# Merged recurrence and gather on TensorE: token transposes in pairs, their use two slots behind

## The chip, the cores and the metric

One core of a Trainium2 chip runs the whole program in one launch. The metric is the time of an execution in microseconds (us) of device time. The kernel before takes 2057.97 us, the median of three runs (2055.84 to 2064.03).

## What is computed

One inference step of a hybrid decoder layer, over a prompt of 1024 tokens and eight sampled sequences with a paged cache of 2048 rows each. Three token mixers stand side by side: a gated linear attention (GLA), a sparse attention with compressed, selected and window branches, and an mLSTM. The stage that is changed does two jobs of it. The first is the GLA recurrence over the prompt:

```python
# S_t = diag(a_t) S_{t-1} + k_t^T v_t,  o_t = q_t S_t, evaluated chunk by chunk
rel = jnp.where(causal, bcum[:, :, :, None, :] - bcum[:, :, None, :, :], -jnp.inf)
scores = jnp.einsum('bhtd,bhsd,bhtsd->bhts', qc, kc, jnp.exp(rel))
o = einsum('bhts,bhse->bhte', scores, vc) + einsum('bhtd,bhde->bhte', qc * exp(bcum), s)
s_new = exp(b_end) * s + einsum('bhsd,bhse->bhde', kc * exp(b_end - bcum), vc)
```

The second prepares the sampled sequences: for each of the eight, the cached rows are gathered through the page table, and every 16 rows of compression keys and values go through the first layer of an MLP (`r @ w1`), and the selection keys are multiplied by the queries.

## The kernel before, in words

The program is a row of stages, each a block in which every engine has its own instruction stream and engines wait for each other on semaphores. The stage of the change is `gla_and_gather` (line 1528), which runs from about 771 to 1036 us. Its order is written out by hand. It loops `it` over eight iterations (`NCH` = 8 chunks of 128 prompt tokens, and at the same time `NS` = 8 sequences), and a short ninth one finishes chunk 7. An iteration has 12 slots `n` (`NFILL`).

What TensorE issues, all in float32:

- `fill(s, n)` (line 1676): four 128x128 transposes of gathered rows of sequence s into PSUM bank `TP[n % 2]`. It waits until the copy of slot n-2 has emptied that bank. For slots 0 and 6 it waits for the gather too.
- The copy out of that bank to `tr[:, n % 4]` is done by ScalarE for slots 0, 2, 4, 5, 6, 7, 8, 10 (line 1776) and by VectorE for 1, 3, 9, 11 (line 1867).
- `use(s, n)` reads what was copied. In slots with n % 6 below 4 it is eight matmuls on 64 rows with the MLP's weights (line 1692, called **use** below); in slots 4, 5, 10, 11 it is four matmuls on 128 rows with only 8 moving columns, the queries (line 1700, called **short use** below). Use 0 of a sequence waits for `hid_ready`: ScalarE copies the sums of the sequence before (`copy_hidden`, lines 1781 and 1782, after its use 11), then VectorE adds to them (`add_hidden`, line 1873).
- `level(c, l)` (line 1717), l from 0 to 7: four matmuls on 64 rows that give one level of chunk c's scores. There is one pair of PSUM banks for them, so level l waits (`sc_used`) until VectorE's `merge` of level l-1 (lines 1848 and 1849) has taken the scores over. Level 0 waits in addition for `queries` of VectorE.
- `turn_keys` (line 1725), `keys_by_values` (line 1731) and `outputs` (lines 1741 and 1743). `outputs` waits for all eight merges.

Before, TensorE takes slot after slot: fill n, then in slots 6 to 11 level n-6 (in slots 0 and 1 levels 6 and 7 of the chunk before), then use n-1. `outputs` of the chunk before stands in slot 3, `turn_keys` in slot 5, `keys_by_values` in slot 8.

VectorE's order matters: after the copy of slot 3 it does `update` (line 1857, needs `outputs`), `queries` (lines 1831 to 1837), the `differences` for the next chunk (lines 1820 to 1825), and then merge 0. In slot 1 it does the copy, `add_hidden`, merge 7. ScalarE has, beside its copies, two exponent passes per chunk. GpSimd multiplies keys and issues the gathers; SyncE stores gathered values to DRAM.

The code of the loop:

```python
for n in range(NFILL if it < NCH else 4):
    if it < NCH:
        fill(it, n)
    if n < 2 and it:
        level(it - 1, n + 6)
    if n >= 6 and it < NCH:
        level(it, n - 6)
    if n and it < NCH:
        use(it, n - 1)
    elif n == 0 and it:
        use(it - 1, NFILL - 1)
```

Of the kernel before, what the change touches and what calls it, by code (L numbers as in the profile page):

```python
# [67 lines left out]
NCH = T // CH  # L68
# [1459 lines left out]
def gla_and_gather(nc, io, keep, at):  # L1528
# [6 lines left out]
    with ExitStack() as ctx:  # L1535
# [22 lines left out]
        NFILL = 12  # L1558
# [3 lines left out]
        def copies(s, n):  # L1562
            own = by_act if n in by_act else by_dve
            return len(own) * s + own.index(n) + 1
# [12 lines left out]
        with nc.Block() as block:  # L1577
# [88 lines left out]
            def _(pe):  # L1666
                def fill(s, n):
                    half, f = n // 6, n % 6
                    if f == 0:
                        pe.wait_ge(gathered[half], 16 * (s + 1))  # L1670
                    if NFILL * s + n >= 2:
                        prior = (s, n - 2) if n >= 2 else (s - 1, n + NFILL - 2)
                        pe.wait_ge(copied_a if prior[1] in by_act else copied_v, copies(*prior))
                    for u in range(4):
                        token = kv[half][:, (f % 2) * 4 + u, f // 2, :, :].rearrange("p h d -> p (h d)")
                        last = nc.tensor.transpose(TP[n % 2][:, u * P:(u + 1) * P], token, ident[:, :])
                    last.then_inc(f_done, 1)

                def use(s, n):
                    half, f = n // 6, n % 6  # L1680
                    pe.wait_ge(copied_a if n in by_act else copied_v, copies(s, n))
                    if f < 4:
                        j = f // 2
                        if n == 0:
                            pe.wait_ge(w_in, 16)
                            if s:
                                pe.wait_ge(hid_ready, s)
                        for u in range(4):
                            r = half * 8 + (f % 2) * 4 + u
                            for h in range(2):  # L1690
                                rws = slice(h * 64, h * 64 + 64)
                                last = nc.tensor.matmul(HID[h][:, j, :], w1[rws, j, r, :, :].rearrange("d w e -> d (w e)"),
                                                        tr[rws, n % 4, u * P:(u + 1) * P],
                                                        start=(j == 0 and r == 0), stop=(h == 1 and j == 1 and r == 15))
                    else:
                        if n == 4:
                            pe.wait_ge(gated, 1)
                        for u in range(4):
                            r = half * 8 + (f - 4) * 4 + u
                            last = nc.tensor.matmul(SCP[:, r * 8:r * 8 + 8], tr[:, n % 4, u * P:(u + 1) * P], qbd[:, s, :],  # L1700
                                                    start=False, stop=r == 15)
                    last.then_inc(f_used, 1)

                def level(c, l):
                    if l == 0:
                        if c == 0:
                            pe.wait_ge(setup, 1)
                        pe.wait_ge(keyed, c + 1)
                        pe.wait_ge(queried, c + 1)
                    if 8 * c + l:  # L1710
                        pe.wait_ge(sc_used, 8 * c + l)
                    for hp in range(HP):
                        for side in range(2):
                            rws = slice(side * 64, side * 64 + 64)
                            k, q = ((zq[rws, c % 2, 2 + hp, :], zq[rws, c % 2, hp, :]) if l == NL else
                                    (kd[c % 2][rws, hp, l, :], dd[c % 2][rws, hp, l, :]))
                            last = nc.tensor.matmul(side_sc[:, side, hp, :], k, q, start=True, stop=True)
                    last.then_inc(sc_done, 1)

                def turn_keys(c):  # L1720
                    pe.wait_ge(keyed, c + 1)
                    if c:
                        pe.wait_ge(g_updated, c)
                    for hp in range(HP):
                        last = nc.tensor.transpose(kt[:, hp * P:(hp + 1) * P], kd[c % 2][:, hp, KEND, :], ident[:, :])
                    last.then_inc(kt_done, 1)

                def keys_by_values(c):
                    pe.wait_ge(kt_copied, c + 1)
                    for hp in range(HP):  # L1730
                        last = nc.tensor.matmul(dl[:, hp * P:(hp + 1) * P], kn[:, hp, :], vnat[:, c, hp * P:(hp + 1) * P],
                                                start=True, stop=True)
                    last.then_inc(dl_done, 1)

                def outputs(c):
                    pe.wait_ge(sc_used, 8 * c + 8)
                    if c:
                        pe.wait_ge(og_copied, c)
                        pe.wait_ge(g_updated, c)
                    for h in range(4):  # L1740
                        nc.tensor.matmul(og[:, h * 64:(h + 1) * 64], pT[:, h % 2, h // 2, :], vnat[:, c, h * 64:(h + 1) * 64], start=(h == 0), stop=False)
                    for hp in range(HP):
                        last = nc.tensor.matmul(og[:, hp * P:(hp + 1) * P], dd[c % 2][:, hp, QIN, :], G[:, hp, :],
                                                start=False, stop=hp == HP - 1)
                    last.then_inc(og_done, 1)

                for it in range(NCH + 1):
                    for n in range(NFILL if it < NCH else 4):
                        if it < NCH:
                            fill(it, n)  # L1750
                        if n < 2 and it:
                            level(it - 1, n + 6)
                        if n >= 6 and it < NCH:
                            level(it, n - 6)
                        if n and it < NCH:
                            use(it, n - 1)
                        elif n == 0 and it:
                            use(it - 1, NFILL - 1)
                        if n == 3 and it:
                            outputs(it - 1)  # L1760
                        if n == 5:
                            turn_keys(it)
                        if n == 8:
                            keys_by_values(it)

            @block.scalar
# [1584 lines left out]
```

## Time and profile before

| | |
|---|---|
| median of three runs | 2057.97 us (2055.84 to 2064.03) |
| the profiled execution, its own time | 2060.44 us |
| its span, first to last instruction | 2058.7 us |
| TensorE matmuls busy | 1810.5 us, 88% |
| VectorE busy | 1115.2 us, 54% |
| ScalarE busy | 636.6 us, 31% |
| mean granted TensorE clock | 0.923 of full speed |

The profile is one execution recorded by the hardware. The 1.7 us between its time and its span lie outside the instructions. The granted clock has two levels: 1.00 is 2.4 GHz and 0.50 is 1.2 GHz; a stretch that holds both shows a value between. In the timeline a row is a run of instructions of one line; a matmul here leaves two records, a transpose one. Ends of matmuls are modelled, so spacings from start to start are the safer measure.

### The profile page before, as it was taken

To read this page: it belongs to the slowest core of one execution; us is meant where nothing else is said; L and a number is where in the kernel's file an instruction comes from. 1 tells how busy PE (TensorE), PEld (TensorE's weight loads), DVE (VectorE), ACT (ScalarE), POOL (GpSimd) and SP (SyncE) were. 2 spreads that over 40 slices of the span, in tenths; PEclk is the share of its full clock that TensorE was granted. 3 is DMA by queue.
4 is the path that set the end of the run, shared out by engine and by line. 5 is a ranking of instruction groups with operands and counts; after the bars stand their busy time and mean duration, and the time that the engine had idled before them with its cause. 6 is when DMAs were issued, how large, how long until landed. Compare 5 with 4: busy or idle time off the path is not lost. (4 is left out here: it accounts for less than half of the span.)

```text
span 2058.7 us, 32209 instructions
## 1 busy us (share of the span) xinstructions
PE 1810.5 (88%) x12919; PEld 1679.4 (82%) x12919; DVE 1115.2 (54%) x1984; ACT 636.6 (31%) x1136; POOL 118.4 (6%) x141
## 2 busy tenths in 40 slices
PE   6989999667888886889974478999999999999997
PEld 5989989656676775777863278999999999999997
DVE  5462662266777663555555765744445544444544
ACT  6513322144554443333223334512121111121111
POOL 0000000000000004132112120000000000000000
PEclk8989999858999997999976679999999999999999
DMA  7631143410000005554464547211111111211102
GB/s 189 87 95 32 52 154 122 112 23 21 11 12 1 1 2 219 191 175 179 140 164 66 174 154 217 77 39 59 41 41 41 41 41 43 79 41 41 41 21 83
DMA packets 172273, 170.87 MB, mean 83 GB/s; under 512 B 49788, under 2 KB 156884, under 8 KB 168452
## 3 DMA queue, kind: packets, MB, share of 16 engines
q1 hardware_dynamic: 168692, 131.54, 22.2%
q0 software_dynamic: 2304, 33.56, 4.3%
q10 hardware_dynamic: 1168, 4.26, 0.9%
q8 instruction: 75, 1.23, 0.3%
q14 instruction: 34, 0.28, 0.0%
HBM read 136.98 MB, written 36.56 MB: 84 GB/s over the span
## 5 line engine op out<-in xcount | busy, mean ns | idle before, releaser
L58 PE MATMUL pm<-hidH,weights 128*128 128x344 f32 x768 | 247.2, 322 | 4.4 <-DVE weights L3166 4.4
L58 PE MATMUL pm<-hH,wuH 128*128 128x344 f32 x768 | 247.1, 322 | 3.1 <-DVE wuL L3161 3.1
L59 PE MATMUL pm<-hidL,weights 128*128 128x344 f32 x768 | 246.3, 321 | 0.0
L60 PE MATMUL pm<-hidH,weights 128*128 128x344 f32 x768 | 246.0, 320 | 0.0
L60 PE MATMUL pm<-hH,wuL 128*128 128x344 f32 x768 | 245.7, 320 | 0.0
L59 PE MATMUL pm<-hL,wuH 128*128 128x344 f32 x768 | 245.6, 320 | 0.0
L58 PE MATMUL pz<-hH,winH 128*128 128x344 f32 x600 | 202.2, 337 | 11.0 <-DVE zb L830 6.5
L59 PE MATMUL pz<-hL,winH 128*128 128x344 f32 x600 | 195.7, 326 | 0.0
L60 PE MATMUL pz<-hH,winL 128*128 128x344 f32 x600 | 195.5, 326 | 0.0
L3170 DVE SCALAR_TENSOR_TENSOR act<-pm,onat 128x344 f32<-128x344 f32 x96 | 49.3, 516 | 245.9 <-PE pm L60 245.7
L3181 DVE TENSOR_TENSOR onat<-pm,onat 128x344 f32<-128x344 f32 x256 | 129.0, 513 | 70.3 <-PE pm L60 70.3
L58 PEld LDWEIGHTS pm<-hidH,weights 128*128 128x128 f32 x768 | 144.8, 189 | 4.7 <-issue 4.7
L58 PEld LDWEIGHTS pm<-hH,wuH 128*128 128x128 f32 x768 | 144.9, 189 | 3.9 <-issue 3.3
L59 PEld LDWEIGHTS pm<-hidL,weights 128*128 128x128 f32 x768 | 145.2, 189 | 0.0
L60 PEld LDWEIGHTS pm<-hidH,weights 128*128 128x128 f32 x768 | 145.0, 189 | 0.0
L60 PEld LDWEIGHTS pm<-hH,wuL 128*128 128x128 f32 x768 | 145.0, 189 | 0.0
L59 PEld LDWEIGHTS pm<-hL,wuH 128*128 128x128 f32 x768 | 144.6, 188 | 0.2
L58 PEld LDWEIGHTS pz<-hH,winH 128*128 128x128 f32 x600 | 116.5, 194 | 15.0 <-issue 13.5
L1362 ACT ACTIVATE pm<-pS,nm 128x640 f32<-128x640 f32 (+7 forms) x128 | 89.5, 701 | 122.4 <-DVE nm L1439 122.4
L3048 ACT ACTIVATE act<-act 128x1032 f32<-128x1032 f32 x32 | 34.1, 1067 | 280.5 <-DVE act L3170 280.5
L3044 ACT ACTIVATE weights<-hs 128x2048 fp32r<-128x2048 f32 x16 | 30.7, 1919 | 286.3 <-PE pm L60 286.3
L59 PEld LDWEIGHTS pz<-hL,winH 128*128 128x128 f32 x600 | 116.3, 194 | 0.9
(592 smaller groups left out, 3556.4 us busy)
## 6 DMA issues: line engine op xcount, KB each, us to landing
uact<-in_w_up_dram SPq DMA_DIRECT2D x16, 1024.0 KB, 6.8
hs<-in_w_down_dram SPq DMA_DIRECT2D x16, 1024.0 KB, 4.9
raw<-in_w_in_dram SPq DMA_DIRECT2D x24, 512.0 KB, 3.9
vS_scratch<-page_rows SPq DMA_DIRECT2D x16, 512.0 KB, 4.8
hold<-vS_scratch SPq DMA_DIRECT2D x8, 1024.0 KB, 12.9
wo<-in_w_out_dram SPq DMA_DIRECT2D x12, 512.0 KB
act<-in_w_out_dram SPq DMA_DIRECT2D x12, 512.0 KB, 3.9
onat<-qkT_scratch SPq DMA_DIRECT2D x18, 256.0 KB, 4.1
```

The source lines that it names most:

```text
L58: nc.tensor.matmul(out, wH, mH, start=(k == 0), stop=False)
L59: nc.tensor.matmul(out, wH, mL, start=False, stop=False)
L60: last = nc.tensor.matmul(out, wL, mH, start=False, stop=(k == n - 1))
L1362: nc.scalar.activation(pm[:, u % 2, g, at:at + w], bank[:, 0:w], ACT.Exp, bias=nm[:, s % 4, 0:1], accum_out=den[:, u % 2, g, branch - 1:br ...
L3044: nc.scalar.activation(wdH[:, :, :], wd[:, :, :], ACT.Copy).then_inc(wdH_ready, 1)
L3048: nc.scalar.activation(act2[:, f, :], act2[:, f, :], ACT.Square)
L3170: nc.vector.scalar_tensor_tensor(out=act2[:, f, cols[third]], in0=ps[third][:, 0:TC], scalar=0.0, in1=rn[:, cols[third]], op0=ALU.max, op1 ...
L3181: nc.vector.tensor_tensor(y, ps[4 + n % 4][:, 0:TC], y, ALU.add).then_inc(added, 1)
```

## The change

TensorE alone gets another order; no instruction is added or taken away, and no other engine's stream is touched. Slots are taken in pairs (0 and 1, 2 and 3, and so on): both fills of the pair come first, into both banks; then level, use, level, use, and the use is that of the slot two behind. `outputs` follows slot pair 2, `turn_keys` pair 4, `keys_by_values` pair 8.

```diff
-                    for n in range(NFILL if it < NCH else 4):
+                    for first in range(0, NFILL if it < NCH else 4, 2):
                         if it < NCH:
-                            fill(it, n)
-                        if n < 2 and it:
-                            level(it - 1, n + 6)
-                        if n >= 6 and it < NCH:
-                            level(it, n - 6)
-                        if n and it < NCH:
-                            use(it, n - 1)
-                        elif n == 0 and it:
-                            use(it - 1, NFILL - 1)
-                        if n == 3 and it:
+                            fill(it, first)
+                            fill(it, first + 1)
+                        for n in (first, first + 1):
+                            if n < 2 and it:
+                                level(it - 1, n + 6)
+                            if n >= 6 and it < NCH:
+                                level(it, n - 6)
+                            if n >= 2 and it < NCH:
+                                use(it, n - 2)
+                            elif n < 2 and it:
+                                use(it - 1, NFILL - 2 + n)
+                        if first == 2 and it:
                             outputs(it - 1)
-                        if n == 5:
+                        if first == 4:
                             turn_keys(it)
-                        if n == 8:
+                        if first == 8:
                             keys_by_values(it)
```

How TensorE's instructions stand, at two places. `page_rows` are gathered rows (fill), `prs` the scores (level), `w_heads` the MLP weights (use), `qbd_n` the queries (short use).

First place, levels 0 to 2 of chunk 1. Before, from `turn_keys` on:

```order
L1725 MATMUL pr<-ident,kd 128x128 x2
L1676 MATMUL pr<-ident,page_rows 128x128 x4
L1717 MATMUL prs<-hold,kd 128x128 x4
L1700 MATMUL pr<-qbd_n,hs 128x8 x4
L1676 MATMUL pr<-ident,page_rows 128x128 x4
L1717 MATMUL prs<-hold,kd 128x128 x4
L1692 MATMUL pr<-hs,w_heads 128x128 x8
L1676 MATMUL pr<-ident,page_rows 128x128 x4
L1717 MATMUL prs<-hold,kd 128x128 x4
L1692 MATMUL pr<-hs,w_heads 128x128 x8
```

With the change:

```order
L1725 MATMUL pr<-ident,kd 128x128 x2
L1676 MATMUL pr<-ident,page_rows 128x128 x8
L1717 MATMUL prs<-hold,kd 128x128 x4
L1700 MATMUL pr<-qbd_n,hs 128x8 x4
L1717 MATMUL prs<-hold,kd 128x128 x4
L1700 MATMUL pr<-qbd_n,hs 128x8 x4
L1676 MATMUL pr<-ident,page_rows 128x128 x8
L1717 MATMUL prs<-hold,kd 128x128 x4
L1692 MATMUL pr<-hs,w_heads 128x128 x8
L1717 MATMUL prs<-hold,kd 128x128 x4
L1692 MATMUL pr<-hs,w_heads 128x128 x8
```

Both fills of slots 6 and 7 now stand ahead of level 0, and only the short use 4 stands between level 0 and level 1; behind level 1 come a short use and eight transposes, where before a full use followed at once.

Second place, around the end of a sequence: levels 6 and 7, use 11, use 0 and `outputs`. Before:

```order
L1676 MATMUL pr<-ident,page_rows 128x128 x4
L1717 MATMUL prs<-hold 128x128 x4
L1700 MATMUL pr<-qbd_n,hs 128x8 x4
L1676 MATMUL pr<-ident,page_rows 128x128 x4
L1717 MATMUL prs<-zq 128x128 x4
L1692 MATMUL pr<-hs,w_heads 128x128 x8
L1676 MATMUL pr<-ident,page_rows 128x128 x4
L1692 MATMUL pr<-hs,w_heads 128x128 x8
L1676 MATMUL pr<-ident,page_rows 128x128 x4
L1692 MATMUL pr<-hs,w_heads 128x128 x8
L1741 MATMUL pr<-hold,pTg 128x64 x4
L1743 MATMUL pr<-Gst,hold 128x128 x2
```

With the change:

```order
L1676 MATMUL pr<-ident,page_rows 128x128 x8
L1717 MATMUL prs<-hold 128x128 x4
L1700 MATMUL pr<-qbd_n,hs 128x8 x4
L1717 MATMUL prs<-zq 128x128 x4
L1700 MATMUL pr<-qbd_n,hs 128x8 x4
L1676 MATMUL pr<-ident,page_rows 128x128 x8
L1692 MATMUL pr<-hs,w_heads 128x128 x16
L1741 MATMUL pr<-hold,pTg 128x64 x4
L1743 MATMUL pr<-Gst,hold 128x128 x2
```

Use 11, the last short one, now stands behind level 7; between it and use 0 there are the eight transposes of slots 2 and 3, and uses 0 and 1 run together just ahead of `outputs`.

## Rows read from the trace of the kernel before

**Rows 1.** Page, part 1: busy time, share of the span, instructions.
```profile
PE 1810.5 (88%) x12919; PEld 1679.4 (82%) x12919; DVE 1115.2 (54%) x1984; ACT 636.6 (31%) x1136; POOL 118.4 (6%) x141
```

**Rows 2.** Windows, the merged stage; columns: PE, PEld, DVE, ACT, POOL busy, granted clock, DMA.
```profile
790.50:1032.70 242.20, 217.19 (x2300) 187.81 (x2300) 129.69 (x298) 78.98 (x116) 51.18 (x21) 0.94 0.47 162
```

**Rows 3.** Waits of TensorE, 775 to 1035 us: in total, times, longest.
```profile
PE prs L1717 <- DVE pTg L1849: 10.7, 7, 1.7
...
PE pr L1692 <- DVE onat L1873: 7.9, 7, 1.1
PE prs L1717 <- issue: 4.1, 7, 0.6
```

**Rows 4.** Timeline, TensorE, 811 to 852 us: start, duration, line, count, idle before.
```profile
818.78 1.68 PE L1692 MATMUL pr<-hs,w_heads 64*128 64x128 f32 x16 [1.12 <-DVE onat L1873]
...
823.70 1.16 PE L1692 MATMUL pr<-hs,w_heads 64*128 64x128 f32 x16
824.79 1.10 PE L1741 MATMUL pr<-hold,pTg 128*128 128x64 f32 x8
825.74 0.66 PE L1743 MATMUL pr<-Gst,hold 128*128 128x128 f32 x4
...
830.60 0.72 PE L1717 MATMUL prs<-hold,kd 64*128 64x128 f32 x8 [0.58 <-issue]
...
834.48 0.71 PE L1717 MATMUL prs<-hold,kd 64*128 64x128 f32 x8 [1.68 <-DVE pTg L1849]
835.02 1.06 PE L1692 MATMUL pr<-hs,w_heads 64*128 64x128 f32 x16
...
842.88 0.66 PE L1676 MATMUL pr<-ident,page_rows 128*128 128x128 f32 x4
843.47 0.72 PE L1717 MATMUL prs<-hold,kd 64*128 64x128 f32 x8
844.11 1.06 PE L1700 MATMUL pr<-qbd_n,hs 128*128 128x8 f32 x8
845.03 0.63 PE L1676 MATMUL pr<-ident,page_rows 128*128 128x128 f32 x4
...
846.24 1.06 PE L1700 MATMUL pr<-qbd_n,hs 128*128 128x8 f32 x8
...
849.55 1.71 PE L1692 MATMUL pr<-hs,w_heads 64*128 64x128 f32 x16 [1.12 <-DVE onat L1873]
```

**Rows 5.** Timeline, VectorE, the same stretch.
```profile
817.78 0.86 DVE L1873 TENSOR_TENSOR onat<-pr,onat 64x254 f32<-64x254 f32 x2
...
826.44 1.16 DVE L1857 SCALAR_TENSOR_TENSOR Gst<-Gst,eb,pr 64x64 f32<-64x64 f32 x4 [1.94 <-PE pr L1743]
...
833.70 0.72 DVE L1849 COPY_PREDICATED pTg<-lvl,prs 128x512 f32<-128x512 uint32 x1
```

**Rows 6.** Timeline, ScalarE, the same stretch.
```profile
816.56 0.77 ACT L1781 ACTIVATE onat<-pr 64x256 f32<-64x256 f32 x2 [1.04 <-PE pr L1700]
```

**Rows 7.** Windows with the granted clock, columns as in rows 2.
```profile
815.90:819.20 3.30, 2.18 (x25) 1.85 (x26) 2.48 (x6) 1.03 (x3) 3.14 (x2) 1.00 0.00 0
819.20:822.70 3.50, 3.50 (x30) 2.95 (x28) 0.41 (x1) 0.60 (x1) 0.04 (x1) 0.51 0.76 253
...
829.50:834.50 5.00, 2.74 (x27) 2.17 (x25) 4.75 (x12) 1.47 (x3) 0.96 (x1) 1.00 0.82 221
```

**Rows 8.** Windows with the granted clock, end of the stage.
```profile
1027.40:1030.80 3.40, 2.94 (x30) 2.52 (x29) 1.34 (x3) 1.02 (x3) 0.00 (x0) 1.00 0.00 0
1030.80:1034.50 3.70, 1.77 (x9) 1.77 (x9) 1.72 (x4) 0.01 (x1) 0.00 (x0) 0.51 0.00 0
```

**Rows 9.** Timeline, TensorE, start of the stage.
```profile
790.55 2.08 PE L1692 MATMUL pr<-hs,w_heads 64*128 64x128 f32 x16 [8.37 <-DMA w_heads<-w1S_scratch]
```

**Rows 10.** Timeline, TensorE, end of the stage.
```profile
1028.02 0.72 PE L1717 MATMUL prs<-hold,kd 64*128 64x128 f32 x8
...
1029.65 0.71 PE L1717 MATMUL prs<-zq 64*128 64x128 f32 x8
```

## The prediction, made before the changed kernel ran

> **What bounds the kernel now.** I read the page first: TensorE is busy for 88% of the span [rows 1], but that is a mean over all stages. The change touches one, so I read the windows of that stage next: 242.2 us, of which TensorE's matmuls are busy for 217.2, VectorE for 129.7, ScalarE for 79.0, at a granted clock of 0.94 [rows 2]. TensorE bounds it, except where its waits stand. The list of waits puts these down to two places per iteration [rows 3]: merge 0 of a chunk (10.7 us in 7 waits, with 4.1 us more ahead of level 0), and `add_hidden` (7.9 us in 7). The timeline then gives one iteration in full [rows 4], and the windows the clock [rows 7, 8].
>
> One iteration lasts 30.77 us (use 0 at 818.78 and again at 849.55). I cut it into four pieces, from start to start:
>
> 1. End of `outputs` (825.74 + 0.66 = 826.40) to level 1 (834.48): 8.08 us [rows 4]. VectorE sets this: its `update` starts at 826.44 and merge 0 ends at 833.70 + 0.72 = 834.42 [rows 5], one thing behind the other. TensorE idles 0.58 + 1.68 = 2.26 us in it.
> 2. Level 1 to use 11 (846.24): 11.76 us, all of it TensorE's own work.
> 3. Use 11 to use 0 (849.55): 3.31 us. ScalarE starts its copies 1.09 us after use 11 (816.56, a cycle earlier) [rows 6], `add_hidden` runs from 817.78 to 818.64 [rows 5], and use 0 starts 0.14 us later. TensorE idles 1.12 us.
> 4. Use 0 to the end of `outputs` (818.78 to 826.40): 7.62 us, of which part runs at the low clock.
>
> The clock is the fourth cost. Soon after use 0 the granted clock falls: 1.00 from 815.9 to 819.2, then 0.51 from 819.2 to 822.7 [rows 7], that is, the 1.2 GHz level for nearly all of it. At full clock piece 4 up to `outputs` would be three uses at 1.09 (823.70 to 824.79) and two fills at 0.59 (842.88 to 843.47), 4.45 us, where the trace has 6.01. So the fall costs 1.56 us, and 10.9 us over the seven iterations that have it. At full clock an iteration would last 29.21 us.
>
> **The change part by part, cycle of 29.21 us.** No instruction is added or removed and only TensorE's order changes, so the costs are waits, switches and the clock.
>
> Piece 1: VectorE's chain starts at the end of `outputs` and has the same links, so level 1 still starts 8.08 us after it. On TensorE both sides of the piece hold four fills, three uses, `turn_keys` and level 0; with the second fill ahead of level 0, the 0.58 us wait there goes, and the one ahead of level 1 grows to about 2.1 us. **Zero.**
>
> Piece 2: it takes in one fill (0.59), one level (0.64) and one short use (0.92) [rows 4]: +2.15 us. Added too is waiting inside the pairs. Now only a use stands between two levels. The nearest row is the end of the stage, where it is so already: level 6 to level 7 takes 1.63 us [rows 10], against 0.64 + 0.92 = 1.56 us of work, so +0.07 us for each of four pairs, 0.28. The lower bound is nothing; the upper is 0.69 more per pair where VectorE's own copy gets between two merges, which its order puts behind the first of them. Against that stand fewer changes between 64-row and 128-row work: 11 round trips per iteration now, 8 then. The row gives use after fill 1.09 us, use after level about 0.99 (835.02 and the fill behind it), so 0.10 us each, −0.3 us. The Trainium skill says that changing the tiling mode drains TensorE (TensorEngine Tiling (Array Packing), Key Properties), with no figure; the sum goes by the row's 0.10. Piece 2 becomes 13.9 us.
>
> Piece 3: ScalarE's copies and `add_hidden` follow use 11 as before; the cover changes from fill 1 and level 7 to fills 2 and 3, both about 1.15 us. VectorE's copy of slot 1 is now done earlier, which frees about 0.06. So 3.25 us, wait about 1.2. Merge 7 still stands behind `add_hidden` on VectorE, but `outputs` comes two uses later: covered.
>
> Piece 4: two fills and one use move out (2 x 0.59 + 1.09 = 2.27), and use 1 directly behind use 0 saves one switch: 6.06 − 2.37 = 3.69 us at full clock.
>
> Sum: 8.08 + 13.95 + 3.25 + 3.69 = about 29.0 us, −0.2 us per iteration, −1.4 in seven. The ends: in iteration 0, fills 2 and 3 move into the 8.37 us wait for the weights [rows 9] and the wait for merge 0 there goes (0.5 us); at the stage's end use 11 stands one level (0.64) later and the last `outputs` waits for it. Together −1.2 us. **Order alone: −2.6 us.**
>
> **The clock** decides the rest, and the trace shows the new situation only in parts. What came before a fall: at 819.2, short uses and levels and then 1.12 us of idling; at 1030.8, short uses and levels with hardly any idling, TensorE busy for 2.94 of 3.40 us, and yet 0.51 afterwards [rows 8]. What came before none: 829.5 to 834.5, with 2.3 us idle, stayed at 1.00 [rows 7]; there a fill stands between the short use and the long wait, and a full use follows at once. With the change short use 4, a wait of 2.1 us, level 1 and short use 5 are neighbours, and in each iteration level, short use, level, short use stand in a row as at the end of the stage. I expect a fall at merge 0's wait in every iteration, dearer than nothing and at most the 1.56 us of today, since part of the slow stretch lies in the wait: 1.4 us, 9.8 in seven. At use 0 a wait of 1.2 us remains; the fall there comes in about four iterations of seven, 1.3 us each, 5.2. That makes 15.0 us, where 10.9 are lost now: +4.1. Bounds: 7 (one cheap fall per iteration) and 21.8 (two full ones), −3.9 and +10.9.
>
> Total −2.6 + 4.1 = **+1.5 us**. The profiled execution's own time, 2060.44 us, would become 2062; it stands 2.5 us above the median of the runs, so against the median 2058.0 I say **2059.5 us**. Other stages keep their instructions; a stage that starts at another moment may lose or gain a clock stretch of the same 1.5 us, which I add to the range.
>
> **Rivals.**
>
> *The falls go away.* The iteration loses its regular 30.77 us, the fills cover the waits, and the clock stays up. Time 2058.0 − 2.6 − 10.9 = 2044.5 us. For it: longer waits than 1.12 us already pass without a fall [rows 7]. Against it: the 2.1 us wait now has light work on both sides.
>
> *The falls multiply.* Level, short use, level, short use, then fills, then a wait: the clock falls there, again at merge 0's wait, and once it is low a weak stretch keeps it low, 2.5 stretches of 1.56 us per iteration, 27.3 us: 2058.0 − 2.6 + 16.4 = 2072 us. It passes 0.5% from about 3.3 us lost per iteration on. For it: the fall at 1030.8 after exactly this pattern [rows 8]. Against it: between 790.5 and 1032.7 the mean clock is 0.94, one fall an iteration, and every low stretch in the cycle ended after one. The Trainium skill speaks for it: transposes, it says, do not bring TensorE to the full clock, as they do not count as busy in the same way (TensorE: Matmul & The Clock Gate, Part 4). By that rule eight in a row would cost as much as idling, and the time would be this rival's. The trace does not bear it out: eight transposes and 2.3 us of idling lie between 829.5 and 834.5 at 1.00.
>
> *The merges become the bound.* If VectorE's copies of slots 1, 9 and 11 each push a merge by 0.69 us that TensorE waits for, seven or eight iterations pay 2.1 us: +15 us, 2073 us. Against it: the copies stand behind the merge that is waited for first.
>
> *Nothing changes* (one fall per iteration at another place) is inside the forecast.
>
> **How the numbers follow.** A measurement of this kernel can tell about 0.5%, 10.3 us, from no change. The forecast gets 0.74 and all of it lies within 0.5%; falls gone 0.12, faster; falls multiplied 0.10 and merges 0.04, slower. Its own bounds are 2058.0 − 2.6 − 3.9 = 2051.5 and 2066.3; other stages and the spread of runs (6 us above the median, 2 below) widen them, and the range reaches some way to both rivals: 2047 to 2070 us.
>
> **What would show it.** Right: `outputs` to level 1 still 8.1 us with one wait of about 2.1; no wait at level 0; levels in a pair 1.6 us apart; use 11 to use 0 3.25 us; iterations of 29 us where no fall lies, 30.5 where one does; a low stretch behind level 1. Wrong: iterations of 29 throughout (first rival), a mean clock under 0.90 in the stage (second), gaps over 2 us from level to level (third), or VectorE's chain itself of another length.

## The result, and the profile of the changed kernel

| | before | changed |
|---|---|---|
| median of nine runs | 2055.56 us (2049.70 to 2064.03) | 2070.55 us (2066.14 to 2080.90) |
| profiled execution's own time | 2060.44 us | 2068.03 us |
| its span | 2058.7 us | 2066.3 us |

The ratio is 1.0081 with a 95% interval of 1.0062 to 1.0100: the changed kernel is 15 us slower. My forecast was no change, 2059.5 us, with a range up to 2070.0; the rival "the falls multiply" had been put at 2072 us and a chance of 0.10. The two profiled executions lie 7.6 us apart, not 15: that of the kernel before took 4.9 us more than its median, that of the changed kernel 2.5 us less.

TensorE on the page, against [rows 1]; then the changed kernel's windows, the first over the whole stage as in [rows 2] (from the first use to the last `outputs`), the others over one iteration. The columns are busy time of PE, PEld, DVE, ACT and POOL, granted clock, DMA share, GB/s:

```profile
PE 1829.7 (89%) x12919; PEld 1703.5 (82%) x12919; DVE 1112.5 (54%) x1984; ACT 634.3 (31%) x1136; POOL 117.9 (6%) x141
```

```profile
788.50:1038.40 249.90, 227.56 (x2292) 206.00 (x2292) 121.77 (x292) 75.87 (x115) 51.08 (x21) 0.85 0.45 156
...
823.40:826.80 3.40, 1.81 (x17) 1.52 (x16) 3.23 (x12) 1.07 (x3) 0.91 (x1) 1.00 0.92 256
826.80:833.60 6.80, 6.12 (x36) 5.56 (x38) 1.49 (x5) 2.10 (x2) 0.42 (x1) 0.50 0.81 308
833.60:847.20 13.60, 12.40 (x150) 11.10 (x148) 6.60 (x17) 5.34 (x8) 5.51 (x2) 1.00 0.09 20
847.20:850.60 3.40, 3.40 (x33) 3.18 (x32) 1.23 (x2) 0.00 (x0) 0.00 (x0) 0.51 0.93 390
```

The stage takes 249.9 us where it took 242.2, at a mean clock of 0.85 where it was 0.94. TensorE's matmuls are busy 10.4 us longer in the stage with the same instructions. Within the iteration shown the clock is at 0.50 from 826.8 to 833.6, twice as long as the low stretch of an iteration before, and again from 847.2 to 850.6. Low time in the whole stage is 76 us, where it was 31. It lies in two places per iteration: a stretch of 3.4 us around use 0 in all seven, and one around level 1 in all seven too, of 6.8 us in six of them and 3.4 in the last. In the kernel before there was only the one at use 0. In these six the fall comes by turns 0.7 us ahead of the start of level 1, inside the wait, and 0.6 us behind it; at use 0 it comes 0.2 us behind the start, or 2.1 us ahead of it, before the wait has begun.

The waits of TensorE, against [rows 3], and its timeline over one iteration, against [rows 4]:

```profile
PE prs L1717 <- DVE pTg L1851: 13.0, 6, 2.2
...
PE pr L1692 <- DVE onat L1875: 5.5, 7, 1.2
```

```profile
818.75 0.66 PE L1743 MATMUL pr<-Gst,hold 128*128 128x128 f32 x4
...
822.47 1.04 PE L1676 MATMUL pr<-ident,page_rows 128*128 128x128 f32 x8
823.61 0.71 PE L1717 MATMUL prs<-hold,kd 64*128 64x128 f32 x8
824.26 1.06 PE L1700 MATMUL pr<-qbd_n,hs 128*128 128x8 f32 x8
827.49 1.22 PE L1717 MATMUL prs<-hold,kd 64*128 64x128 f32 x8 [2.17 <-DVE pTg L1851]
828.64 1.87 PE L1700 MATMUL pr<-qbd_n,hs 128*128 128x8 f32 x8
830.36 1.95 PE L1676 MATMUL pr<-ident,page_rows 128*128 128x128 f32 x8
832.24 1.23 PE L1717 MATMUL prs<-hold,kd 64*128 64x128 f32 x8
...
843.20 0.71 PE L1717 MATMUL prs<-zq 64*128 64x128 f32 x8
843.85 1.06 PE L1700 MATMUL pr<-qbd_n,hs 128*128 128x8 f32 x8
844.76 1.07 PE L1676 MATMUL pr<-ident,page_rows 128*128 128x128 f32 x8
847.03 3.62 PE L1692 MATMUL pr<-hs,w_heads 64*128 64x128 f32 x32 [1.20 <-DVE onat L1875]
850.59 1.13 PE L1741 MATMUL pr<-hold,pTg 128*128 128x64 f32 x8
```

Read it by the pieces of the prediction. End of `outputs` (818.75 + 0.66 = 819.41) to level 1 at 827.49 is 8.08 us, as before; the wait ahead of level 1 is 2.17 us and there is none ahead of level 0 (823.61). Around it stand short use, wait, level, short use, transposes, and there the rows nearly double: short use 828.64 to 830.36 takes 1.72 us instead of 0.92, eight transposes 1.88 instead of 1.0. Use 11 (843.85) to use 0 (847.03) is 3.18 us. From use 0 to `outputs` two uses take 3.56 us (to 850.59); at full clock they would take about 2.0.

### The profile page after: what moved, and what is told of

Same layout as the page of the kernel before. It is cut to its first block and busy times, and to the rows that moved or that the text cites. A ratio compares the mean times of both kernels' runs of the same rounds, so it can differ in the third digit from the quotient of the medians.

```text
span 2066.3 us, 32209 instructions
## 1 busy us (share of the span) xinstructions
PE 1829.7 (89%) x12919; PEld 1703.5 (82%) x12919; DVE 1112.5 (54%) x1984; ACT 634.3 (31%) x1136; POOL 117.9 (6%) x141
## 5 line engine op out<-in xcount | busy, mean ns | idle before, releaser
L58 PEld LDWEIGHTS pz<-hH,winH 128*128 128x128 f32 x600 | 115.9, 193 | 15.0 <-issue 13.5
```

The lines of the kernel that those rows point to most:

```text
L58: nc.tensor.matmul(out, wH, mH, start=(k == 0), stop=False)
```

## The experiments

Twelve kernels ran, ten of them variants and two the kernels themselves once more. "Stage" is the time from the first use to the start of the last `outputs` in the profiled execution, "low" the time in it at the 1.2 GHz level, "ratio" that of the runs to those of the kernel before on the same chip (whose medians there were 2057.1 to 2058.5 us for e1 to e10, 2055.56 us for the changed kernel). "Profiled" is the time of the execution that stage and low are read from; it can lie some us off the median, and stages are rounded by themselves. Where the text says by how many us a kernel beats the changed one, the two medians can be from different chips; the ratios are the safer measure.

| kernel | median, us | ratio (95%) | profiled, us | stage, us | low, us |
|---|---|---|---|---|---|
| before | 2055.56 | | 2060.44 | 242.2 | 31 |
| changed | 2070.55 | 1.0081 (1.0062 to 1.0100) | 2068.03 | 249.9 | 76 |
| e1 changed, waits fed | 2047.80 | 0.9949 (0.9931 to 0.9967) | 2050.82 | 230.0 | 15 |
| e2 before, waits fed | 2056.73 | 0.9991 (0.9978 to 1.0003) | 2050.07 | 235.1 | 13 |
| e3 single slots, use two behind | 2076.49 | 1.0091 (1.0075 to 1.0107) | 2082.84 | 266.0 | 82 |
| e4 pairs, use one behind | 2055.86 | 1.0006 (0.9992 to 1.0020) | 2055.64 | 237.7 | 26 |
| e5 short uses together | 2043.19 | 0.9926 (0.9909 to 0.9943) | 2049.45 | 229.3 | 48 |
| e6 changed, fed with transposes | 2046.81 | 0.9958 (0.9946 to 0.9971) | 2048.06 | 229.5 | 18 |
| e7 e5 with its wait fed | 2041.15 | 0.9926 (0.9911 to 0.9941) | 2041.75 | 218.8 | 11 |
| e8 changed, fed elsewhere | 2086.82 | 1.0158 (1.0131 to 1.0186) | 2082.05 | 267.3 | 66 |
| e9 changed, merge 0 first | 2043.78 | 0.9925 (0.9910 to 0.9939) | 2045.62 | 233.1 | 52 |
| e10 e5, merge 0 first | 2037.27 | 0.9900 (0.9885 to 0.9915) | 2037.27 | 217.8 | 30 |
| c1 before, once more | one execution | | 2059.75 | 243.3 | 35 |
| c2 changed, once more | one execution | | 2062.75 | 251.3 | 77 |

**The theory**: the order itself is no slower; the loss is TensorE's clock, which falls where waits and light work (short uses, levels) stand together. **The rival**: the new order costs by itself, in waits or in its spacing.

### Feed the waits with idle matmuls

```diff
+def warm(n):
+    for _ in range(n):
+        nc.tensor.matmul(og[:, 256:384], ident[:, :], ident[:, :], start=True, stop=True)
...
+warm(7)    # ahead of level 1, iterations 1 to 7
 level(it, 1)
...
+warm(4)    # ahead of use 0
 use(it, 0)
```

> The changed kernel, with idle matmuls of TensorE (a product of the identity with itself into the unused half of the outputs' bank, read by nobody) put into its two waits: seven ahead of level 1, four ahead of use 0, in iterations 1 to 7. They add 11 matmuls per iteration, about 1.9 and 1.1 us, less than the waits of 2.17 and 1.2 us. Clock theory (the changed kernel loses 3.4 us per iteration to the 1.2 GHz level, because light work stands around its waits): the low stretches go, iterations come down from 32.4 us to 29 to 30 us, the time falls by 16 to 24 us against the changed kernel, to 0.5% below the kernel before or better. Rival (the new order itself costs: levels too close, use behind use, a longer chain): the clock stays up but the time stays within 5 us of the changed kernel or rises.

The windows of the stage and the timeline around level 1:

```profile
790.70:1020.70 230.00, 222.06 (x2447) 200.95 (x2447) 122.78 (x294) 75.88 (x115) 49.15 (x21) 0.97 0.50 171
```

```profile
856.12 1.06 PE L1700 MATMUL pr<-qbd_n,hs 128*128 128x8 f32 x8
857.04 1.81 PE L1706 MATMUL pr<-ident 128*128 128x128 f32 x14
859.36 0.72 PE L1721 MATMUL prs<-hold 64*128 64x128 f32 x8 [0.51 <-DVE pTg L1860]
860.00 1.06 PE L1700 MATMUL pr<-qbd_n,hs 128*128 128x8 f32 x8
```

It came out as the theory says: 2047.80 us, 22.8 us under the changed kernel (ratios 0.9949 and 1.0081) and 0.5% under the kernel before, with 11 more matmuls in each of seven iterations. The stage is 19.9 us shorter at a clock of 0.97. The feed (857.04) lies where the wait was; what is left of it is 0.51 us, and the short use and the fills behind level 1 run at their full-clock times again. Iterations without a low stretch last 28.53 us from `outputs` to `outputs`. So this is what the new order takes at full clock.

In two of the seven iterations a low stretch of 3.4 us is left, and no wait stands ahead of it. The windows ahead of one, and over it:

```profile
869.70:873.90 4.20, 4.20 (x42) 3.76 (x41) 1.38 (x4) 0.60 (x1) 4.05 (x2) 1.00 0.00 0
873.90:877.30 3.40, 3.40 (x18) 3.40 (x17) 1.91 (x5) 1.52 (x4) 0.88 (x1) 0.50 0.53 159
```

Ahead of it stand eight transposes, level, short use, level, short use, with TensorE busy for all of the 4.20 us, and the clock falls all the same. So the theory needs one correction: this work can bring a fall without a wait, here in two iterations of seven. In the changed kernel the fall at use 0 came in all seven, in three of them ahead of the wait too (878.0, 942.8 and 1007.7).

The same in the kernel before (two ahead of level 0, five ahead of level 1, four ahead of use 0; the idle matmuls ahead of the levels wait for `og_copied` first):

> The kernel before, with the same idle matmuls in its waits: two ahead of level 0, five ahead of level 1, four ahead of use 0. Clock theory: its one low stretch per iteration (1.56 us) goes, iterations of 30.77 us become 29.2 us, the time falls by about 9 to 11 us, 0.5% under the kernel before. Rival (the clock is no lever here): within 3 us of the kernel before, or slower by the matmuls that do not fit.

The window of its stage, columns as above:

```profile
782.90:1018.00 235.10, 227.61 (x2455) 199.40 (x2455) 129.83 (x298) 78.98 (x116) 51.22 (x21) 0.97 0.48 167
```

A miss by half. The stage came down by 7.1 us and its undisturbed iterations last 29.2 us, both as expected. But the median fell by too little to be told from nothing (ratio 0.9991). The profile shows where part of it went: the rest of the program, from the last `outputs` on, took 1030.3 us, where it took 1026.0. What made that rest longer is not shown. The profiled execution itself is 6.7 us quicker than the median of this kernel's runs; it reached the stage 7.6 us earlier (782.9 against 790.5), with the same work ahead.

### Fill the same work in elsewhere

```diff
+warm(11)    # ahead of level 2, iterations 1 to 7
 level(it, 2)
```

> The counter test to the first experiment: the changed kernel with its 11 idle matmuls per iteration at a place where TensorE does not wait, ahead of level 2. Clock theory: the waits and the light work around them are as in the changed kernel, so both low stretches stay; the matmuls add 2.75 us to each of seven iterations, 19 us: about 2090 us, 1.7% over the kernel before. If any further matmul helped, wherever it stands, the time would fall or stay.

The window of its stage:

```profile
787.00:1054.20 267.20, 243.34 (x2446) 222.82 (x2446) 123.02 (x294) 76.06 (x115) 46.85 (x21) 0.88 0.42 147
```

16.3 us slower than the changed kernel; the added matmuls alone were estimated at 19 in the expectation. The low time stays high, at 66 us: around level 1 the stretches of 6.8 us stay in six iterations. At use 0 only two of seven are left, with waits of 1.2 us as before, where I had expected all of them. The gain of the first experiment came from where the matmuls stand.

### Feed with transposes

> The changed kernel with its waits filled as in the first experiment, but with transposes of the identity (14 and 8, about the same time) in place of matmuls. If transposes count as little for the clock as the Trainium skill says (TensorE: Matmul & The Clock Gate, Part 4), the low stretches stay and the time is that of the changed kernel, within 5 us. If they count, it falls as with the matmuls, by about 20 us, to 0.5% under the kernel before.

The window of its stage:

```profile
789.60:1019.10 229.50, 221.14 (x2447) 199.33 (x2447) 122.79 (x294) 75.87 (x115) 49.45 (x21) 0.96 0.49 171
```

2046.81 us, the same as with matmuls, and the same clock (0.96). Transposes hold the clock up here as well as matmuls do. The Trainium skill says that they do not count as TensorE being busy in the same way (TensorE: Matmul & The Clock Gate, Part 4). This run, with float32 transposes at 0.96, does not bear that out. Whether transposes alone would lift the clock from its low level is not shown by any run.

### One half of the change at a time

Single slots, the use two behind:

```diff
-if n and it < NCH:
-    use(it, n - 1)
-elif n == 0 and it:
-    use(it - 1, NFILL - 1)
+if n >= 2 and it < NCH:
+    use(it, n - 2)
+elif n < 2 and it:
+    use(it - 1, NFILL - 2 + n)
```

> Half of the change alone: slots one by one as before, but the use is that of the slot two behind. Short uses 4 and 10 now stand behind levels 1 and 7, and the wait for merge 0 comes between fill 7 with short use 4 still ahead of it in slot 6. Clock theory: what matters is how light the work around the waits is; fills still separate level and short use, so one to one and a half low stretches per iteration, the time within 6 us of the kernel before. Rival (use two behind is what costs): as slow as the changed kernel, 0.8% over.

Its stage windows, then TensorE around level 1 and ahead of use 0:

```profile
787.80:1053.70 265.90, 240.68 (x2296) 207.39 (x2296) 129.76 (x298) 77.61 (x115) 46.85 (x21) 0.85 0.42 147
```

```profile
865.80 0.82 PE L1717 MATMUL prs<-hold 64*128 64x128 f32 x8 [1.69 <-DVE pTg L1849]
866.55 1.87 PE L1700 MATMUL pr<-qbd_n,hs 128*128 128x8 f32 x8
868.28 1.09 PE L1676 MATMUL pr<-ident,page_rows 128*128 128x128 f32 x4
...
880.70 1.06 PE L1700 MATMUL pr<-qbd_n,hs 128*128 128x8 f32 x8
881.61 0.64 PE L1676 MATMUL pr<-ident,page_rows 128*128 128x128 f32 x4
882.18 0.71 PE L1717 MATMUL prs<-zq 64*128 64x128 f32 x8
882.82 1.06 PE L1700 MATMUL pr<-qbd_n,hs 128*128 128x8 f32 x8
883.74 0.63 PE L1676 MATMUL pr<-ident,page_rows 128*128 128x128 f32 x4
886.01 1.43 PE L1692 MATMUL pr<-hs,w_heads 64*128 64x128 f32 x16 [1.65 <-DVE onat L1873]
```

My expectation failed; the one I gave to the rival ("use two behind is what costs") held: 0.9% slower, low for 82 us. The low stretches lie at two places now. One is level 1, where the kernel before had no low stretch: six iterations of seven have one of 6.8 us, which begins 0.2 to 0.6 us behind its start (865.80). Behind it a short use now follows and no longer a full use. The wait ahead is as long as before, 1.69 us against 1.68 [rows 4], and the work ahead of the wait is no lighter (a use stands where a short use stood). So why the clock falls here and did not before is not shown. The other place is use 0. Ahead of it stand short use, fill, level, short use, fill and then a wait of 1.65 us; in the kernel before the last short use had a fill and level 7 behind it, and the wait was 1.12 us [rows 4]. Use 11, whose end starts the chain over ScalarE and VectorE to use 0, has moved behind level 7, so one level less covers that chain.

Pairs, the use one behind (the diff is the above in reverse, inside the pair loop):

> The other half of the change alone: fills in pairs, but each use only one slot behind, as before. Short use 11 then stands behind level 6 and use 0 directly behind level 7, ahead of fills 2 and 3. Waits: 3.25 us from use 11 to use 0 with 0.9 + 0.6 us of cover, about 1.7 us; between `outputs` and level 1 two short uses, so a wait of about 1.2 to 1.5 us for merge 0. Lag theory (the use two behind carries the loss, because it brings level and short use together around the waits): near the kernel before, within 5 us. Pair theory (both fills first carries it): 0.8% over the kernel before, like the changed kernel.

Its stage windows and waits:

```profile
788.70:1026.40 237.70, 211.23 (x2300) 188.39 (x2300) 126.93 (x298) 77.21 (x116) 48.99 (x21) 0.95 0.47 165
```

```profile
PE prs L1717 <- DVE pTg L1851: 12.4, 6, 2.2
PE pr L1692 <- DVE onat L1875: 10.4, 7, 1.5
```

As expected by the lag theory: the same as the kernel before (1.0006). The waits of 2.17 us are the same as in the changed kernel, and those at use 0 are longer (10.4 us in all against 5.5), yet there are six low stretches of 3.4 us in seven iterations, three behind level 1 and three at use 0, and not two per iteration. So the length of the wait does not decide alone whether the clock falls. Behind level 1 stands a full use here, and a short use with eight transposes there. That can't bring a fall that comes ahead of level 1, as in the changed kernel, but it goes with how long the stretch lasts: 3.4 us in all three here, 6.8 us in all six in the changed kernel and in e3. That the full use is what ends it sooner is likely; no run moves it by itself.

### Take the wait away

```diff
-if n == 6 and it + 1 < NCH:
-    differences(it + 1, range(4, 9)).then_inc(diffs, 1)
 if n >= 6:
     merge(it, n - 6)
+if n == 6 and it + 1 < NCH:
+    differences(it + 1, range(4, 9)).then_inc(diffs, 1)
```

> The changed kernel with one thing moved on VectorE: merge 0 comes ahead of the second half of the next chunk's differences (about 2.0 us), so level 1 may start 2 us earlier, 6.1 us after `outputs`, and the wait of 2.17 us is all but gone. No matmul is added. Clock theory (a low stretch needs the light work and the wait together): the low stretch behind level 1 goes in most iterations, iterations of 27 to 29 us, 25 us or more under the changed kernel, of which 14 us are the waits themselves. If light work alone brings the low level (as at the stage's end), only the 14 us come: 2056 us, near the kernel before.

The window of its stage, and then its waits:

```profile
781.50:1014.70 233.20, 218.36 (x2293) 197.29 (x2293) 122.98 (x294) 75.86 (x115) 45.68 (x21) 0.89 0.49 169
```

```profile
PE pr L1692 <- DVE onat L1875: 7.6, 7, 1.2
...
PE prs L1717 <- DVE pTg L1851: 2.1, 4, 0.6
PE prs L1717 <- issue: 1.2, 2, 0.6
```

26.8 us under the changed kernel: the waits ahead of level 1 went from 13.0 to 3.3 us (two of them the profile puts down to `issue`), and low time from 76 to 52 us. The expectation held in size, but the low stretches only thinned out: eleven, where there were sixteen. Four of them still lie behind level 1, after waits of 0.4 to 0.6 us, and four at use 0, whose waits of up to 1.2 us this edit leaves as they were.

### Short uses together, and the best version

```diff
 for n in (first, first + 1):
+    late = first in (0, 6) and n == first + 1
-    if n >= 6 and it < NCH:
+    if n >= 6 and it < NCH and not late:
         level(it, n - 6)
     if n >= 2 and it < NCH:
         use(it, n - 2)
...
+    if late and n >= 6 and it < NCH:
+        level(it, n - 6)
```

Levels 6 and 7 of the chunk before are treated alike.

> The changed kernel with two levels moved: level 1 behind short uses 4 and 5 instead of between them, and level 7 behind short uses 10 and 11. 0.9 us of work moves into the wait for merge 0, and 0.6 us into the wait ahead of use 0, so at full clock an iteration should last 29.0 - 1.5 = 27.5 us. Order theory (the waits are what counts): 10 us less than the changed kernel, or more. Clock theory: the light work around merge 0's wait is the same or lighter, the two low stretches per iteration stay, and the gain of 1.5 us per iteration comes in part: 5 to 10 us less than the changed kernel; if the low stretches grow to three, nothing is gained.

The window of its stage, then one ahead of a low stretch and one over it:

```profile
786.30:1015.70 229.40, 216.53 (x2293) 194.73 (x2293) 122.38 (x293) 76.65 (x115) 48.67 (x21) 0.89 0.49 171
893.00:896.60 3.60, 3.60 (x37) 3.17 (x36) 1.36 (x3) 1.19 (x3) 3.45 (x2) 1.00 0.00 0
896.60:900.00 3.40, 3.40 (x24) 3.07 (x24) 2.29 (x5) 1.04 (x3) 0.81 (x1) 0.50 0.54 159
```

2043.19 us: 27.4 us less than the changed kernel, of which I expected 5 to 10, or 10 or more under the order theory. The stage fell by 20.6 us. The moved work (1.5 us in each of seven iterations) is worth about 11 of it, and the low time fell too, from 76 to 48 us, where I had warned that the low stretches might stay or grow. So this run alone would speak for the order theory; that the clock is the lever rests on the fed runs and on e8. The fall at 896.6 comes behind level, two short uses, level, with TensorE busy for all of the 3.60 us before: here too no wait was needed.

With four idle matmuls ahead of that late level 1:

```diff
 if late and n >= 6 and it < NCH:
+    if it:
+        warm(4)
     level(it, n - 6)
```

> The kernel with the short uses together, plus four idle matmuls (1.0 us) in its wait of 1.28 us for merge 0. Its iterations last 26.9 to 30.6 us, the longer ones with low stretches. Clock theory: iterations of 27 to 28 us, 7 to 15 us less than without the idle matmuls, about 1.2% under the kernel before. Order theory: no difference.

The stage fell by another 10.5 us to iterations of 26.9 to 27.8 us, as expected, at a low time of 11 us. The time did not follow: the median is 2.0 us lower and the ratio is that of e5, 0.9926, where I had expected 1.2% under the kernel before, so no gain over e5 is shown. Part of the gap is that the profiled execution of e5 is the slowest of its five (2049.45 us, 6.3 over the median); part is the rest of the program, 1034.3 us here and 1032.1 in e5.

And e5 with VectorE's move of e9 (merge 0 ahead of the second half of the differences), and no idle matmul:

> The same move on VectorE in the kernel with the short uses together. Its wait for merge 0 was 1.28 us; level 1 comes behind both short uses at 6.9 us after `outputs` at the earliest, so 1.2 us per iteration go, 8 us in all, and the low stretches with them: 2030 to 2038 us, 1.0 to 1.3% under the kernel before. If the low stretches stay, 2036 to 2042 us.

The window of its stage, and then one row of its waits:

```profile
788.10:1005.90 217.80, 209.10 (x2292) 188.09 (x2292) 122.74 (x294) 76.63 (x115) 45.86 (x21) 0.93 0.52 180
```

```profile
PE pr L1676 <- DMA page_rows<-in_cache_nsa_kv_dram,idx: 3.7, 3, 2.0
```

2037.27 us, 1.0% under the kernel before (0.9885 to 0.9915), the lowest of all. Each of the two moves alone gave 0.7%. No wait for merge 0 is left, and yet low stretches stay (30 us in all), four of them around a level 1 that waits for nothing. The result lies in both of the ranges that I gave. This is the version to keep. What is late next is the gather: fills now wait for it, which in the changed kernel they did not behind the first use.

### The two kernels once more

> The kernel before, profiled once more. The clock's falls depend on where an execution happens to lie, so the stage need not take the 242.2 us from first use to last `outputs` again: 236 to 243 us, with four to nine low stretches, if the first profile was one of its slower executions; 242 us again if seven falls are its rule.

> The changed kernel, profiled once more: 249.9 us from first use to last `outputs` in its first profile, with two low stretches in most iterations. If that is its rule, 247 to 253 us again; the difference of the medians (15 us) then comes from the kernel before being usually below its profile, and from the stage behind.

The kernel before: stage 243.3 us, again with iterations of 30.76 us and one fall in each. The changed kernel, the window of its stage:

```profile
783.10:1034.40 251.30, 229.09 (x2293) 207.45 (x2293) 122.83 (x294) 75.88 (x115) 48.71 (x21) 0.85 0.45 156
```

Stage 251.3 us, iterations of 32.0 and 32.9 us in turn. The pattern came back in both, so it is not an accident of one execution, and my guess that the first profile of the kernel before had a slow stage was wrong. The stage's difference is 8 us in both pairs. The whole executions are only 3.0 us apart this time (2062.75 and 2059.75 us), because this one reached the stage 6.3 us earlier (783.1 against 789.4), with the same work ahead.

## Why the prediction was wrong

The forecast of +1.5 us was counted from 2058.0 us, the median of three runs; nine runs give 2055.56. As a difference the miss is 13.5 us.

**Piece 1, zero: right.** 8.08 us, no wait at level 0, 2.17 us at level 1 (predicted 2.1).

**Pieces 2 to 4: right, and a little too dear.** At full clock the iteration lasts 28.53 us (the fed kernel), where I had 29.0; most of it is piece 2, 13.66 us where I had 13.95. Levels in a pair stand 1.60 to 1.64 us apart, as in [rows 10]; use 11 to use 0 is 3.18 us (predicted 3.25). The third rival, the merges as the bound, did not come: no such wait is in the list.

**The clock: the term that failed.** I put its loss at 15.0 us: a fall at merge 0's wait in every iteration at 1.4 us, and one at use 0 in four of seven at 1.3, with an upper bound of 21.8 from two full falls. That is 2.1 us per iteration, with a bound of 3.1. Measured, the six steady iterations average 32.43 us, 3.9 over the full-clock 28.53: 23.4 us in these six alone, beyond the bound for seven. Two things were mis-sized. Falls at use 0 came in all seven iterations. And the fall at level 1's wait brought a low stretch of 6.8 us in six iterations of seven, not one of 3.4: I had priced each fall as the one that the trace of before showed. The bound of "two full falls" was no bound. The mean clock of the stage, 0.85, is the sign that I had named for the second rival (under 0.90).

**The weighing of the rivals.** The fall at 1030.8 [rows 8] was the nearest row to the new pattern (level, short use, level, short use), and I gave what it says a chance of 0.10, because longer waits in the old order passed without a fall [rows 7]. A wait that passed once was no sign: in e3 all five waits of the same 1.7 us are met by a fall. With pairs alone, where the full use behind level 1 stays, nothing is lost; with the lag alone 0.9% is. The rival's loss of 2.5 stretches of 1.56 us, 3.9 us per iteration, is what was measured. That its time, 2072 us, is so near the measured 2070.55 is in part luck: by its sum the stage would have grown by 13.8 us, and in the profile it grew by 7.7.

**The rule of the Trainium skill** (TensorE: Matmul & The Clock Gate, Part 4) pointed to the right side for a reason that this case does not bear out: by it transposes are not busy time as matmuls are, and yet feeding with them raised the clock of the stage from 0.85 to 0.96.

**What stays open.** That the stage loses its time to the clock is shown by the fed runs and e8. What brings each single fall is not: falls come with and without a wait, and in one order a wait passes that in another does not.

The stage accounts for 8 of the 15 us between the medians. The rest is in no profile that I have. In the first pair of profiles the changed kernel gains 2.0 us ahead of the stage and loses 1.9 behind it; in the second pair it gains 6.3 ahead and loses 1.4 behind. Both parts have the same instructions in both kernels, but for eight transposes that the changed one does ahead of its first use instead of behind it. The time ahead of the stage moves from one execution to another of the same kernel: the changed one reached its first use at 788.5 us and at 783.1.

The same holds behind the stage, where the mLSTM recurrence starts at the low clock and leaves it sooner or later. The windows of its first part, before, in the second profile of the changed kernel and in e7:

```profile
1032.70:1077.40 44.70, 34.88 (x211) 29.81 (x212) 22.93 (x60) 11.14 (x34) 9.13 (x38) 0.68 0.66 178
```

```profile
1034.40:1076.60 42.20, 32.11 (x211) 27.29 (x212) 22.93 (x60) 11.11 (x34) 9.12 (x38) 0.73 0.71 189
```

```profile
1005.00:1059.40 54.40, 45.79 (x210) 40.06 (x212) 23.51 (x62) 11.11 (x34) 9.13 (x38) 0.50 0.64 156
```

The same 210 or so records take 44.7 us at 0.68, 42.2 at 0.73 and 54.4 at 0.50. In the first profile of the changed kernel they take 49.2, so this part alone differs by 7.0 us between two executions of one kernel, and it can't be put down to the order alone. In e5, e7 and e10 they take 54.4 each, 9.7 us more than before; these three share the late levels 1 and 7. In e7 and e10 the program gains 16 and 21 us by its medians, and the stage 23 and 24. Whether that order brings it, or the moment at which the stage ends, is not shown.

## What to carry to other kernels

Before reordering an engine's work around a wait, look at the granted clock on both sides of it and at what stands there: in this kernel the same wait of 2.17 us went with 26 us of low time in one order (e4) and 76 in another, and a tidy order that gathers the light instructions there can cost more than it saves. A bound for the clock's cost must allow low stretches to last longer than those in the trace of before. Moving work into the wait and shortening the other engine's chain gave 0.7% each and 1.0% together, where the order alone lost 0.8%.

## What the runs showed that I had not expected

- Transposes of the identity fed into the waits hold the clock as well as matmuls do: 0.96 against 0.97 over the stage, 2046.81 us against 2047.80.
- Adding 11 idle matmuls to each of seven iterations makes the changed kernel 22.8 us faster if they stand ahead of its waits, and 16.3 us slower if they stand where it does not wait.
- The clock fell with TensorE busy without a gap: 4.20 of 4.20 us in e1 and 3.60 of 3.60 in e5, over levels and short uses.
- The same 1.7 us of wait ahead of level 1 passed at full clock in all six iterations of the kernel before that have it, and all five of its kind met a fall with each use one slot later.
- Each use one slot later, with the same instructions and the same fills, loses 0.9% by itself: low time in the stage rises from 31 to 82 us.
- The first part of the next stage, the mLSTM, took from 42.2 to 54.4 us with the same instructions, at a clock of 0.73 to 0.50; two executions of the changed kernel took 42.2 and 49.2.
